# A hybrid decoder step on one core: the order of the first loads and of the work ahead of the u batches

## What is computed

```python
mod = einsum('nd,de->ne', silu(c), ada_w) + ada_b            # 12 column blocks of 512
sh1, sc1, g1, sh2, sc2, g2 = split(mod, 6)
h = rmsnorm(x, norm1_g) * (1 + sc1) + sh1
z = h @ w_in                                                 # columns [q | k | v | u]
# S5 branch on u: one complex diagonal state for each of 32 groups of 16 channels
abar = exp(lam * dt); bbar = (abar - 1) / lam * b
h_t = abar * h_(t-1) + bbar u_t ; y = Re(c h_t) + d * u      # then gelu, glu
# attention on q, k, v (prompt and cached); output projection; gated residual; mixture of experts
```

## Time and profile before

| | us |
|---|---|
| three timed runs | 855.9, 858.05, 858.37 (median 858.05) |
| the profiled execution: its time | 857.07 |
| its span | 855.1 |
| granted TensorE clock, mean | 0.90 |

### The profile page before, as it was taken

How to read it: one execution, slowest core, us unless ns; L and a number is a source line. 1 busy time by engine, 2 the same in 40 slices (tenths; PEclk the granted TensorE clock), 3 DMA queues, 4 the chain that set the end, 5 groups by cost and what they waited for, 6 DMA issues and landing times.

```text
span 855.1 us, 11967 instructions
## 1 busy us (share of the span) xinstructions
PE 674.8 (79%) x4870; PEld 392.6 (46%) x4870; DVE 288.5 (34%) x683; ACT 180.1 (21%) x364; POOL 139.2 (16%) x229
## 2 busy tenths in 40 slices
PE   2196899999998779797996269958799999979600
PEld 1166888888862344353555244413344444323200
DVE  4847396761110444302554621101000111100048
ACT  3221311222234544431121000100100101100132
POOL 4300005558300133200000010000000000000072
PEclk9988999999999699978986569989799999999955
DMA  9946277564857587877516138999998639999462
GB/s 336 271 147 232 71 240 266 166 253 146 226 118 294 224 346 264 326 233 203 184 56 236 40 121 292 322 391 406 398 372 298 226 127 387 395 400 400 184 208 104
DMA packets 92909, 211.88 MB, mean 248 GB/s; under 512 B 8540, under 2 KB 15084, under 8 KB 92565
## 3 DMA queue, kind: packets, MB, share of 16 engines
q1 hardware_dynamic: 81878, 182.48, 60.0%
q0 software_dynamic: 4976, 18.37, 7.1%
q10 hardware_dynamic: 6000, 10.25, 3.2%
HBM read 197.42 MB, written 18.91 MB: 253 GB/s over the span
## 4 chain that ended last, share of the span: by engine, by line
PE 63%; DVE 11%; SPq 9%; DMA 7%; ACT 4%; issue 4%; POOL 2%; ACTq 0%; DVEq 0%; POOLq 0%
PE ps L2386 14%; PE ps L2002 10%; PE ps L2426 9%; SPq L623 6%; PE ps L1891 5%; PE ps L2301 5%; DMA whalf<-in_w_down 4%; PE ps L1972 4%; PE ps L1897 2%; SPq L588 2%; PE ps L2202 2%; PE ps L2090 1%; PE ps L2115 1%; PE ps L2225 1%; PE ps L2139 1%
## 5 line engine op out<-in xcount | busy, mean ns | idle before, releaser
L2386 PE MATMUL ps<-whalf,xgT 128*128 128x512 f32 (+2 forms) x576 | 173.9, 613 | 17.5 <-DMA whalf<-in_w_up 13.2
L2386 PEld LDWEIGHTS ps<-whalf,xgT 128*128 128x128 f32 (+2 forms) x576 | 67.1, 158 | 116.5 <-issue 111.6
L2426 PE MATMUL ps<-whalf,aT 128*128 128x512 f32 (+2 forms) x288 | 88.2, 634 | 12.7 <-DMA whalf<-in_w_down 10.8
L2002 PE MATMUL ps<-hT,ring 128*128 128x272 f32 x384 | 91.4, 394 | 0.0
L2002 PEld LDWEIGHTS ps<-hT,ring 128*128 128x128 f32 x384 | 71.8, 190 | 15.2 <-issue 1.4
L2301 PE MATMUL ps<-ring,mixT 128*128 128x512 f32 x128 | 60.6, 633 | 5.5 <-DVE pt L1614 5.5
L2426 PEld LDWEIGHTS ps<-whalf,aT 128*128 128x128 f32 (+2 forms) x288 | 33.4, 160 | 60.5 <-issue 58.1
L766 POOL DMA_INDIRECT xg<-h_d,gidx x12 | 11.5, 956 | 244.3 <-PE ps L1891 210.9
L2301 PEld LDWEIGHTS ps<-ring,mixT 128*128 128x128 f32 x128 | 25.6, 204 | 38.8 <-issue 32.4
L750 POOL TENSOR_TENSOR Sb<-Sb,stat 128x128 f32<-128x128 f32 (+3 forms) x32 | 22.4, 720 | 110.4 <-DVE stat L1564 110.4
L1786 DVE COPY ysb<-ps 128x512 f32<-128x512 f32 x12 | 8.3, 692 | 91.8 <-PE ps L2426 91.8
(11 more groups left out here) (395 smaller groups left out, 958.2 us busy)
## 6 DMA issues: line engine op xcount, KB each, us to landing
whalf<-in_w_up SPq DMA_DIRECT2D x32, 1024.0 KB, 14.4
whalf<-in_w_down SPq DMA_DIRECT2D x32, 1024.0 KB, 15.4
whalf<-in_w_gate SPq DMA_DIRECT2D x32, 1024.0 KB, 11.8
ada_half<-in_ada_w SPq DMA_DIRECT2D x16, 1024.0 KB, 5.2
ring<-in_cache_k SPq DMA_DIRECT2D x8, 1792.0 KB, 7.7
ring<-in_cache_v SPq DMA_DIRECT2D x6, 2048.0 KB, 10.1
ring<-in_ada_w SPq DMA_DIRECT2D x4, 2048.0 KB, 16.5
ring<-in_w_in SPq DMA_DIRECT2D x4, 2048.0 KB, 10.9
```

Source lines behind the costliest of these rows:

```text
L2002: ins = mm(ps[:, z % 2, 0:2 * NCOL], r[:, 512 * k + P * (c % 4):512 * k + P * (c % 4 + 1)], hT[:, k, 2 * h:2 * h + 2, :].rearrange("p a b ...
L2386: ins = mm(out[cols, :], xgT[b][:, k, cols], r[:, 512 * (k % 4):512 * (k % 4 + 1)], start=k == 0, stop=k == KD - 1, **tile_at(m_, n))
L2426: ins = mm(ps[cols, 6 + n2, :], aT[:, t % 2, c, cols], r[:, c0:c0 + 512], start=c == 0, stop=c == 3, **tile_at(m_, n))
```

## The change

SP queues `par`, the two bias loads, the identity part of `const`, and x in two pieces ahead of a0; `modrow` comes in pieces by rows, those of the first chunks before a1; a3 and U come before `ct`, `oh`, the rest of `const`, the rest of `modrow` and `h0`. VectorE scales x before the parameter chain, whose power blocks take in mod chunks 0 to 2. TensorE does h_t(0), h_t(1), ada(0), h_t(2) to h_t(4), ada(1) to ada(3). Decode bias and the turning of the input blocks go behind `ada_half(2)`, and `km_in` behind `ada_half(3)`. Waits are changed to match (`x0` for the first two tiles, `parl` for `par`, `init` 32, `modl` 128, `ctl` 128).

```diff
-CS, GSB, DBIAS, HMD, CQ3, CQ4, TABLES, KMD, SSN = range(1, 10)
-GP, DBP, MODTP, ATTSP = range(1, 5)
+CS, GSB, HMD, CQ3, CQ4, DBIAS, TABLES, KMD, SSN = range(1, 10)
+GP, MODTP, DBP, ATTSP = range(1, 5)
 # SP
+        def modrows(a, b, done):
+            for j in range(4):
+                sp.dma_start(modrow[32 * j:32 * j + 32, a:b, :].rearrange("p a b -> p (a b)"),
+                             I["modrow"][j, P * a:P * b].partition_broadcast(32)).then_inc(done, 16)
+        n0 = CCOL["ident"][1]
         sp.dma_start(cT[:, :, :], I["cT"]).then_inc(s("cld"), 16)
-        sp.dma_start(par[:, :], I["par"]).then_inc(s("init"), 16)
-        fill("a0", ada_col(0))
+        sp.dma_start(par[:, :], I["par"]).then_inc(s("parl"), 16)
         sp.dma_start(ctab33[:, :], I["tab33"]).then_inc(s("init"), 16)
         sp.dma_start(ohp[:, :], I["oh_prompt"]).then_inc(s("init"), 16)
-        sp.dma_start(const[:, :], I["const"]).then_inc(s("init"), 16)
-        sp.dma_start(xt[:, 0:QT, :], xq_v).then_inc(s("x"), 16)
+        sp.dma_start(const[:, 0:n0], I["const"][:, 0:n0]).then_inc(s("x0"), 16)
+        sp.dma_start(xt[:, 0:2, :], xq_v[:, 0:2, :]).then_inc(s("x0"), 16)
+        sp.dma_start(xt[:, 2:QT, :], xq_v[:, 2:QT, :]).then_inc(s("x"), 16)
         sp.dma_start(xt[0:NS, QT, :], I["x"][SEQ:NTOK, :]).then_inc(s("x"), 16)
+        fill("a0", ada_col(0))
+        modrows(0, 4, s("modl"))
+        modrows(N_ADA, N_ADA + 4, s("modl"))
         fill("a1", ada_col(1))
+        fill("a2", ada_col(2))
+        sp.wait_ge(s("ada"), 1)
+        fill("a3", ada_col(3))
+        sp.wait_ge(s("ada"), 2)
+        fill("U", win_col(3))
         for n, name in enumerate(("ct_re", "ct_im")):
             sp.dma_start(cq[n][:, :, 0, :], I[name]).then_inc(s("ctl"), 16)
         sp.dma_start(oh[:, :], I["oh_decode"]).then_inc(s("ctl"), 16)
-        for j in range(4):  ... modrow as a whole, to "modl"
-        fill("a2", ...) ; wait ada 1 ; fill("a3", ...)
+        sp.dma_start(const[:, n0:], I["const"][:, n0:]).then_inc(s("ctl"), 16)
+        modrows(4, N_ADA, s("ctl"))
         sp.dma_start(h0[:, 0, :, :], I["h0_re"]).then_inc(s("h0"), 16)
         sp.dma_start(h0[:, 1, :, :], I["h0_im"]).then_inc(s("h0"), 16)
-        sp.wait_ge(s("ada"), 2)
-        fill("U", win_col(3))
 # ACT: g_d store ahead of the squares; squares and evictions of hT in one loop
+        for j in range(NT):
+            if j == 0:
+                act.wait_ge(s("x0"), 32)
+            if j == 2:
+                act.wait_ge(s("x"), 32)
+            ... Square, root of tile j
+            if j >= 2:
+                raw_half(j - 2)
+        raw_half(NT - 2)
+        raw_half(NT - 1)
 # ACT, u batches
         mod_chunk(4)
-        km_out()
         u_out(2)
+        for n in range(8): ... wait btT, evict bp
         u_out(3)
         mod_chunk(5)
         mod_store(4)
+        km_out()
 # VectorE: gsb copy, scaling of x and raw_half moved from behind the parameter
 # chain to behind ts_(q_(4), ...), ahead of dve.wait_ge(s("par_act"), 5)
         for m in range(1, CT):
             ...
             tt_(bpow[m][1][:, :, :], bt1[:, :, :], bt2[:, :, :], ALU.add).then_inc(s("bpow"), 1)
+            mod_chunk(m - 1)
 # VectorE, behind the scaling of hT
+        skip copies (d4)
+        dve.wait_ge(s("ctl"), 128)
+        negate cq_im; next_cq(1); next_cq(2)
         next_cq(3)
         dve.sem_inc(s("dve_prep"), 1)
         next_cq(4)
         dve.sem_inc(s("dve_prep"), 1)
+        dve.wait_ge(s("pe_prep"), DBP)
+        dbias, nbias
         dve.sem_inc(s("dve_prep"), 1)
 # TensorE
-        pe.wait_ge(s("init"), 64)
+        pe.wait_ge(s("init"), 32)
         ... gsb matmuls
         pe.wait_ge(s("dve_prep"), CS)
+        h_t(0)
+        h_t(1)
         ada(0)
-        for j in range(NT):
-            h_t(j)
+        h_t(2)
+        h_t(3)
+        h_t(4)
         ada(1)
-        decode bias, turns of bpad
         ada(2)
         ada(3)
 ...
         u_in(0)
         ada_half(0)
         u_in(1)
         ada_half(1)
+        u_in(2)
+        ada_half(2)
+        dec_bias()
+        bp_t()
+        u_in(3)
+        ada_half(3)
         km_in()
-        for b in range(2, 6):
-            u_in(b)
-            ada_half(b)
+        u_in(4)
+        ada_half(4)
+        u_in(5)
+        ada_half(5)
```

More of the change, by code:

```diff
@@ L655, in _ @@
         pool.sem_inc(s("pool_prep"), 1)
-        pool.wait_ge(s("init"), 64)
+        pool.wait_ge(s("init"), 32)
         for t in range(TDEC):
@@ L669, in _ @@
         pool.sem_inc(s("pool_prep"), 1)
-        pool.wait_ge(s("modl"), 64)
+        pool.wait_ge(s("modl"), 128)
+        pool.wait_ge(s("ctl"), 128)
         def mod_chunk(c):
@@ L838, in _ @@
         for j in range(NT):
[L839 to L844, removed]
+            if j == 0:
+                act.wait_ge(s("x0"), 32)
+            if j == 2:
+                act.wait_ge(s("x"), 32)
+            w = TW[j]
+            f(xsq[0:w, :], xt[0:w, j, :], ACT.Square,
+              accum_out=stat[0:w, j:j + 1]).then_inc(s("sq"), 1)
+            act.wait_ge(s("sq"), j + 1)
+            root(j, j + 1, w, D).then_inc(s("rt"), 1)
+            if j >= 2:
+                raw_half(j - 2)
+        raw_half(NT - 2)
+        raw_half(NT - 1)
         act.wait_ge(s("pe_prep"), MODTP)
@@ L914, in _ @@
         mod_chunk(4)
-        km_out()
         u_out(2)
+        for n in range(8):
+            b, q = n // 4, n % 4
+            act.wait_ge(s("btT"), n + 1)
+            f(bp[b][:, 4 * q:4 * q + 4, :], ps[:, 4 + n % 2, :].rearrange("p (a b) -> p a b", a=4), ACT.Copy)\
+                .then_inc(s("btTe"), 1)
         u_out(3)
@@ L1272, in _, with rstd, raw_half, mod_chunk @@
         ts_(q_(4), q_(4), 3.1415925, -3.1415925, ALU.min, ALU.max).then_inc(s("par_dve"), 1)
+        dve.wait_ge(s("pe_prep"), GP)
+        v.tensor_copy(gsb[:, :], ps[0:HEADS, 6:8, :].rearrange("p a b -> p (a b)")[:, 0:640]).then_inc(s("dve_prep"), 1)
+        def rstd(j, w, width, n):
+            dve.wait_ge(s("sq"), n)
+            dve.wait_ge(s("rt"), n)
+            o(v.reciprocal(stat[0:w, 56 + j:57 + j], stat[0:w, 16 + j:17 + j]))
+        def raw_half(j):
+            dve.wait_ge(s("hTp"), 2 * j + 2)
+            bank = ps[:, 3 + 2 * (j % 2), 0:4 * TW[j]]
+            if j < QT:
+                ins = v.tensor_copy(hT[:, 4:8, j, NSEQ:NCOL], bank.rearrange("p (a b) -> p a b", a=4))
+            else:
+                for k in range(4):
+                    ins = v.tensor_copy(hT[:, 4 + k, :, 0:NSEQ].rearrange("p j n -> p n j"),
+                                        bank[:, NS * k:NS * (k + 1)].rearrange("p (n j) -> p n j", j=TDEC))
+            ins.then_inc(s("hTd"), 1)
+        for j in range(NT):
+            w = TW[j]
+            rstd(j, w, D, j + 1)
+            ts_(xt[0:w, j, :], xt[0:w, j, :], stat[0:w, 56 + j:57 + j], None, ALU.mult).then_inc(s("h"), 1)
+            if j:
+                raw_half(j - 1)
+        raw_half(NT - 1)
+        def mod_chunk(c):
+            dve.wait_ge(s("ada"), c + 1)
+            if c == 0:
+                dve.wait_ge(s("modl"), 128)
+            m = modsb[:, c, :]
+            if c < 2:
+                tt_(m, ps[:, c % 2, 0:P], modrow[:, c, :], ALU.add).then_inc(s("modd"), 1)
+            else:
+                o(stt(out=m, in0=ps[:, c % 2, 0:P], scalar=1.0, in1=modrow[:, c, :], op0=ALU.add, op1=ALU.add))
+                tt_(m, m, modrow[:, N_ADA + c % 2, :], ALU.mult).then_inc(s("modd"), 1)
         dve.wait_ge(s("par_act"), 5)
@@ L1328, in _ @@
         tt_(a4i[:, :], mag4[:, :], s4[:, :], ALU.mult).then_inc(s("par_dve"), 1)
[L1329 to L1371, removed]
         def next_cq(t):
@@ L1382, in next_cq @@
             o(tt_(cq[1][:, :, t, :], cq1[:, :, :], cq2[:, :, :], ALU.subtract))
[L1384 to L1395, removed]
         mod_chunk(3)
@@ L1932, in _ @@
         pe.wait_ge(s("dve_prep"), CS)
+        h_t(0)
+        h_t(1)
         ada(0)
[L1934 to L1935 removed]
+        h_t(2)
+        h_t(3)
+        h_t(4)
         ada(1)
[L1937 to L1941, removed]
[L1942 to L1945 removed]
+        ada(2)
+        ada(3)
         pe.wait_ge(s("hTa"), NT)
         pe.wait_ge(s("hTd"), NT)
[L1948 to L1951, removed]
[L1952 to L1956 removed]
         for c in range(4):
@@ L2038, in _, with bp_t, dec_bias @@
         pe.wait_ge(s("dve_prep"), HMD)
+        def bp_t():
+            pe.wait_ge(s("pool_prep"), BPAD)
+            for n in range(8):
+                b, q = n // 4, n % 4
+                if n >= 2:
+                    pe.wait_ge(s("btTe"), n - 1)
+                for r_ in range(4):
+                    ins = tr(ps[:, 4 + n % 2, P * r_:P * (r_ + 1)], bpad[b][:, 4 * q + r_, :])
+                ins.then_inc(s("btT"), 1)
+        def dec_bias():
+            pe.wait_ge(s("ctl"), 128)
+            pe.wait_ge(s("pool_prep"), PADT)
+            pe.wait_ge(s("dve_prep"), GSB)
+            for b, (c0, c1) in enumerate(((0, 512), (512, DK))):
```

(4 more changed lines are left out.)

35 lines of the change are left out of this document (12 added, 23 removed).

## The result

| | before | after |
|---|---|---|
| median of 20 timed runs each, us | 857.42 | 859.97 |
| profiled execution: time, us | 857.07 | 862.29 |
| its span, us | 855.1 | 860.4 |
| granted clock, mean | 0.90 | 0.89 |
| busy PE / DVE, us | 674.8 / 288.5 | 680.0 / 290.8 |

The ratio after to before is 1.0033, 95% interval 1.0018 to 1.0048: the kernel became some 2.8 us slower (1.5 to 4.1; the two medians of the table lie 2.6 apart), about the smallest difference that a measurement of it can tell from none. The forecast was 858.2, with a range up to 863.0. The size came out nearly as forecast, but two terms of the sum were too small (the time from the first u batch to the tables, and the restart), and the experiments show that the same new front, with the moved groups in another place, makes the kernel some 8 us faster than the change as built.

The account below looks back on a forecast made before the run. TensorE ran nearly without a gap; the VectorE chain kmp, tables, turn_in(0), x_in(1) had 5.1 us of slack and would bind. Saving 1.5 at x_in(1) and losing 1.6 by restart gave +0.1: 858.2 us, range 853.3 to 863.

Parts of the forecast that it names:

- First loads and squares: Front: x's first tiles landed at 8.3 us, a0 at 16, h_t(0) at 12.5, VectorE through with x at 23.5.
- Parameter chain: VectorE from 23.5: 19.6 us plus 1.8 for mod chunks, last chunk at 44.9, first u batch at 49.3 instead of 73.67.
- Moved behind it: Ahead of the tables: moved groups 14.0 us, u batches 2 and 3 14.0; tables start at 102.4, 3.6 later than before.
- What that does: Tables to x_in(1) 28.95 us as before; x_in(1) at 131.35, TensorE waiting 8.9, 1.5 saved.
- The restart: TensorE behind the new wait at x_in(1): 1.6 us lost, half of a slow stretch of 3.23 us at clock 0.50.
- Sum: Whole kernel: -1.5 at x_in(1) plus 1.6 for the restart gives +0.1 us, 858.2 against the median.
- B: Front or moved work quicker: tables at 98.9, x_in(1) at 127.8, 3.4 us saved after the restart, 854.7; chance 0.22.
- C: TensorE behind u_in(0) waits for a late first ada half; with 6 us of delay 862.5; chance 0.16.
- margin of 1.7 us: First ada half, behind u_in(0): there at 54.7, wanted at 56.4, so costed at nothing; each us beyond paid in full.
- D: Small modrow pieces cost their number: 5.5 us more at half of 190 GB/s, half late by 3.8, 862.0; chance 0.06.
- E: Lead kept at x_in(1) if the tables did not bind: 10.3 us, 847.7; chance 0.04 together with others.
- F: x part still held by a late load: last chunk no earlier than a3 allows, 42 us; no time of its own.

Follow-up runs that it names:

- km_early: Changed kernel with decode bias, turned input blocks and km_in together right behind ada_half(1): 851.62 us, ratio 0.9944 to the kernel before.
- moves_only: Kernel before with only decode bias, turned blocks and km_in moved as in the change, its loads and front kept: 866.06 us, ratio 1.0107.
- filler: Changed kernel with 16 unread matmuls into an unused bank filling TensorE's wait ahead of x_in(1): 857.36 us, ratio 1.0010 to the kernel before.
- nodiag_after: Changed kernel without the 16 km diagonal operations on VectorE (4.29 us): 853.99 us, ratio 0.9960 to the kernel before.
- q_late: Changed kernel with the 2 MB load of Q queued behind the next two ada halves: 857.05 us, ratio 1.0007 to the kernel before.
- combo: km_early plus 14 fourth-power-of-A operations moved behind the scaling of hT, and Q's load late as in q_late: 848.43 us, ratio 0.9907.
- combo_split: combo with the decode bias in two halves, behind ada_half(0) and ada_half(1), as in split: 845.29 us, ratio 0.9864 to the kernel before.
- split: km_early with the decode bias in two halves, behind ada_half(0) and ada_half(1): 847.54 us, ratio 0.9893 to the kernel before.

## Why the prediction came out as it did

**The mechanism was right.** The chain km_in, tables, first batch, x_in(1) binds. It was shown from four sides: its own wait in the trace, km_early (taken away, -7.6), the pair without the diagonal (-6.3 and nothing), moves_only (+9.2). That the time came out within 2 us of the forecast is in part luck: errors of both signs stand in the steps, and the profiled execution, at 862.29, is 4 above it. By its own steps:

- *First loads and squares.* First scaling at 12.16 and h_t(0) at 13.06, forecast near 11.5 and 12.5; VectorE through with x at 23.60, forecast 23.5. Two errors cancel there: a0 landed at 17.9 and not at 16, and ada(0) took 1.95 and not the 3.64 of the earlier trace rows.
- *Parameter chain.* Last chunk at 44.08, forecast 44.9; first u batch 48.46, forecast 49.3. 0.8 better in this execution; in filler, nodiag_after and q_late, whose code is the same up to there, it started at 49.66, 50.58 and 50.43 (and ada(0) took 3.64 in the first two). The tables started at 104.85 and 106.19 in filler and nodiag_after, within 1.1 of the changed kernel's.
- *Moved behind it.* Decode bias and turns together 13.93 (76.82 to 90.75), forecast 14.0. The term that was too small is the one carried over from before: first u batch to tables was put at 53.1 us and took 56.6 (55.2 in filler, 55.6 in nodiag_after). u_in(0) to ada_half(1) took 21.7 and not 15.8. Of these 5.9, 3.9 are the stops (4.97 against 1.11) and most of the rest a slow stretch, 3.1 us at 0.54. The later batches and `km_in` gave 2.4 back (13.25 for u batches 2 and 3, put at 14.0; `km_in` 7.7 where before it took 9.3 with its stop). I had read these durations where the loads soon ended beside them (4 GB/s in the second line of the earlier trace rows); in their new place, beside a full queue (279 GB/s from 48 to 58, 392 behind it), they weren't the same.
- *What that does.* Tables to x_in(1) 29.16, put at 28.95; TensorE's wait 8.97, put at 8.9. Both are met. So the tables' start at 105.08 instead of 102.4 is passed on in full: x_in(1) at 134.24, not at 131.35. The 1.5 that were to be saved became 1.4 lost.
- *The restart* was mis-sized: 1.6 by a wait of 4 us, 2.9 measured, with 5.96 us at 0.50 behind a wait of 9. (26.72 us from x_in(1) to y_out(0), 23.78 before.) The filler bears it out in the trace. Nothing in the profile of before showed such a wait ahead of this work; I had taken the price of a wait half as long for the longer one.
- *Sum.* -0.8 from the front, +3.5 to the tables, +0.2 from there to x_in(1), +1.3 from the restart: 4.2 above the forecast +0.1, and +4.3 is what x_in(2) and y_out(0) show. The medians say +2.8 (1.5 to 4.1). The executions scatter by the clock in the attention as shown; whether the other 1.5 are that scatter, or something is given back, isn't settled. moves_only doesn't settle it either: its x_in(2) is 11.9 late (155.90) and its time only 9.2 above, but in the profiles all of that difference arises in the one stretch of the attention in which the profile of before is the long one (12.0 late ahead of it, 9.2 behind it).

**The rivals.** B (854.7, quicker front or moved work): the front was quicker by 0.8, the moved groups weren't; its sum did not come. C (first ada half late): TensorE did not wait, but the margin of 1.7 us did not hold. The half was issued at 46.60 and took 10.7 us to land, so it was there at 57.3: 2.6 later than the 54.7 of the sum (SP came free 1.6 later, and the flight took 10.7 and not 9.7), and 0.9 later than 56.4, where I had TensorE want it. TensorE came for it at 57.70 only because u_in(0) had a stop of 1.98 us just before its end; without the stop it would have waited there for an estimated 1.6 us (57.3 less 55.7). So removing that stop alone would have gained little: the late load stood right behind it. SP was held as feared, yet shorter (SP's timeline after):

```profile
28.65 4.42 SPq L498 DMA_DIRECT2D cq_re<-in_ct_re  x1
33.11 8.85 SPq L498 DMA_DIRECT2D cq_im_negated<-in_ct_im  x1
...
46.60 0.98 SPq L512 DMA_DIRECT2D ada_half<-in_ada_w  x2
```

One hold of 9 us and one of half that, against the earlier trace rows; SP was free at 46.60. In combo and combo_split, whose u batches start at 46, TensorE does wait there, for 2.17 and 1.97 us. VectorE's wait for `ctl` lasted 3.40 us, to 54.48, and was harmless as forecast. D (small pieces cost their number) fell for the eight early pieces. They landed from 17.4 to 19.7, and the stretches around a0's end are these:

```profile
14.00:16.00 2.00, 2.00 (x11) 2.00 (x10) 1.21 (x4) 1.97 (x6) 0.00 (x0) 1.00 1.05 388
16.00:18.00 2.00, 0.82 (x8) 0.42 (x10) 1.81 (x4) 1.93 (x7) 0.00 (x0) 1.00 1.10 293
18.00:20.00 2.00, 2.00 (x66) 1.80 (x66) 0.30 (x1) 0.29 (x1) 0.00 (x0) 1.00 1.04 321
20.00:22.00 2.00, 1.74 (x16) 1.50 (x14) 1.06 (x3) 1.19 (x2) 0.00 (x0) 1.00 1.05 386
```

Against 387 GB/s, 4 us at 293 and 321 lack 0.32 MB, an estimated 0.8 us. The Trainium skill (DMA: Bandwidth & Descriptors, Bandwidth) would have had 64 KB pieces at 0.95 us each, an estimated 7.6 us; for pieces queued one behind the other, between large loads, this trace does not agree with it. The four late pieces moved among other small loads, of which the last landed at 54.4; from 48.46 to 54.00 the rate was about 200 GB/s, near the 190 of the sum. E (the lead kept) was excluded by the tables, but a reorder gets part of it: it is km_early. F: x was scaled at 12.16, so it does what it says.

**What I missed.** I forecast that a wait of 9 us would appear and weighed only its cost, while the sum said at once what to do about it: `kmp` 4 is the first link, and a front that gains 25 us should be spent on it. The changed kernel's order delays the one product of TensorE for which another engine has 29 us of work.

## What to carry to other kernels

When TensorE's order is changed, list for every product what another engine must still do with it before TensorE needs that engine again. Work with a long tail elsewhere (here 29 us of tables) goes first, work without one last; an earlier start of the stage is otherwise just a longer wait. A duration read from a quiet stretch can be too short for the same instructions beside a full load queue (here 15.8 us became 21.7), and a new idle time ahead of TensorE can cost more than itself: here 2.9 us behind 9.

## What the runs showed of the hardware

The clock fell without idleness. In the decode bias (matmuls with 33 rows, TensorE busy throughout) it is granted at 0.50 from the later half on in the changed kernel (82.6 to 89.0), as it was before, and from 77 on in km_early. Half of it, eight matmuls in a row, ran through at 1.00 in split and combo_split (3.06 us each). The slow stretch behind a wait was 3.2 us after 4 us of waiting, 5.96 us after 9, and in the attention, whose code is the same in all kernels, about 10 us in one execution and under 4 in another. A stop of 2 us was followed by one too: 3.1 us at 0.54 after the 1.98 in the changed kernel's first u batch. The stops named "issue" in the first u batches were 2.85 to 4.97 us in three executions with Q in flight beside them and 1.72 in one without.
